# Hybrid encoder step in three-pass fp32r: projection units of 512 columns, halved first loads, gate rows spread by a DMA

## The reference, cut to what matters

```python
xn = rmsnorm(x, g);  z = xn @ w_in                    # qk, v, o, i, f, u, gv, mq, gates
mem_k, mem_v = rmsnorm(mem, g) @ w_k, rmsnorm(mem, g) @ w_v      # 256 memory rows, outputs too
h  = mlstm(silu(conv(qk)), v, i, f)                   # 4 heads, exponential gates, blocks in time
br_mlstm = (norm(h) * sigmoid(o)) @ w_br_mlstm
br_gmlp  = (gelu(u) * spatial(layernorm(gelu(gv)))) @ w_br_gmlp
br_mem   = attention(mq, mem_k, mem_v) @ w_br_mem
x  = x + (sum of sigmoid(gate_b) * br_b) @ w_out
y  = rmsnorm(x + hier_moe(rmsnorm(x)))                # top 1 of 4 groups, top 2 of 8 experts
```

## Time and profile before

| | |
|---|---|
| median of 3 runs | 876.8 us (875.28 to 878.03) |
| profiled execution | 878.86 us, span 876.9 us, mean granted clock 0.981 |
| busy | PE 847.6 us (97%), DVE 592.2 (68%), ACT 481.1 (55%), POOL 61.0 (7%) |
| DMA | 185.8 MB, 212 GB/s over the span |
| expert part | from about 575 us to the end |

### The profile page before, as it was taken

The page is one execution under the profiler, slowest core; times in us unless marked ns, Lnnn a source line. Parts: engine busy times, 40 slices in busy tenths (PEclk is TensorE's granted clock), DMA queues, the critical chain, the costliest instruction groups (busy, mean ns, idle before and its releaser), DMA issues. The chain is left out here.

```text
span 876.9 us, 12973 instructions
## 1 busy us (share of the span) xinstructions
PE 847.6 (97%) x5153; PEld 768.6 (88%) x5153; DVE 592.2 (68%) x837; ACT 481.1 (55%) x647; POOL 61.0 (7%) x126
## 2 busy tenths in 40 slices
PE   5999999999999999999999999999999999999993
PEld 5998989999989998999999998988888788878872
DVE  5665477763345536686555456379889989899883
ACT  4564467754433234454333344437777968877862
POOL 3302011020011011000000000010000000010010
PEclk9999999999999999999999999879999999999997
DMA  9757343334444434445436453559999999999960
GB/s 260 221 161 267 108 139 125 116 96 131 137 132 133 144 120 169 122 126 189 134 120 213 151 190 140 178 183 357 368 341 355 369 386 374 367 369 366 362 238 17
DMA packets 100212, 185.82 MB, mean 212 GB/s; under 512 B 5625, under 2 KB 71441, under 8 KB 100145
## 3 DMA queue, kind: packets, MB, share of 16 engines
q1 hardware_dynamic: 95280, 171.47, 57.2%
q0 software_dynamic: 4064, 11.79, 4.0%
q10 hardware_dynamic: 800, 1.66, 0.5%
HBM read 177.76 MB, written 7.92 MB: 212 GB/s over the span
## 5 line engine op out<-in xcount | busy, mean ns | idle before, releaser
L1356 DVE TENSOR_TENSOR unit_r<-arena,unit_r 128x2048 fp32r<-128x2048 f32 x63 | 144.8, 2299 | 140.8 <-ACT unit_r L966 140.6
L1365 DVE TENSOR_TENSOR w_r<-arena,w_r 128x2048 fp32r<-128x2048 f32 x96 | 217.0, 2287 | 27.9 <-ACT w_r L977 27.9
L570 PE MATMUL pj<-xn_r,unit_r 128*128 128x320 f32 x1536 | 235.0, 311 | 0.0
L570 PEld LDWEIGHTS pj<-xn_r,unit_r 128*128 128x128 f32 x1536 | 225.5, 188 | 5.7 <-issue 3.6
L874 PE MATMUL pj<-w_r,xg 128*128 128x512 f32 x768 | 192.3, 400 | 0.2 <-ACT xg L1206 0.2
L977 ACT ACTIVATE w_r<-arena 128x2048 fp32r<-128x2048 f32 x96 | 180.5, 1913 | 1.2 <-DMA arena<-in_w_exp_up 0.7
L874 PEld LDWEIGHTS pj<-w_r,xg 128*128 128x128 f32 x768 | 143.0, 190 | 31.2 <-issue 0.3
L966 ACT ACTIVATE unit_r<-arena 128x2048 fp32r<-128x2048 f32 x63 | 120.1, 1906 | 24.8 <-PE pj L570 20.0
L903 PE MATMUL pj<-w_r,hidT 128*128 128x512 f32 x384 | 93.5, 392 | 2.7 <-DVE hidT L1719 2.0
L903 PEld LDWEIGHTS pj<-w_r,hidT 128*128 128x128 f32 x384 | 71.6, 188 | 20.1 <-DVE w_r L1365 3.7
L570 PE MATMUL pj<-br_r,unit_r 128*128 128x320 f32 x384 | 59.6, 311 | 0.0
(11 more groups left out here) (359 smaller groups left out, 819.0 us busy)
## 6 DMA issues: line engine op xcount, KB each, us to landing
arena<-in_w_in SPq DMA_DIRECT2D x40, 1024.0 KB, 5.2
arena<-in_w_exp_gate SPq DMA_DIRECT2D x64, 512.0 KB, 4.8
arena<-in_w_exp_up SPq DMA_DIRECT2D x64, 512.0 KB, 6.2
arena<-in_w_exp_down SPq DMA_DIRECT2D x64, 512.0 KB, 5.4
arena<-in_w_mem_v SPq DMA_DIRECT2D x4, 1024.0 KB, 6.4
arena<-in_w_br_mem SPq DMA_DIRECT2D x4, 1024.0 KB, 4.9
arena<-in_w_br_mlstm SPq DMA_DIRECT2D x4, 1024.0 KB, 4.9
arena<-in_w_br_gmlp SPq DMA_DIRECT2D x4, 1024.0 KB, 5.0
```

What stands on the lines that cost most here:

```text
L570: last = mm(bank_of(s)[0:out_rows, 0:out_cols], l, r, start=k == 0, stop=k == len(pairs) - 1)
L1356: v.tensor_tensor(unit_r[n % RING][:, 1, :], ringw[:, n % RING, :], unit_r[n % RING][:, 0, :], ALU.subtract).then_inc(u_lo, 1)
L1365: v.tensor_tensor(w_r[u % NS][:, 1, :], raw_w[u % NS], w_r[u % NS][:, 0, :], ALU.subtract).then_inc(m_lo, 1)
```

## The change

- `memk`, `memv`, `v` and `gv` have units of 512 rows by 512 columns, still 1 MB (a third entry in `UNITS` is the half of the rows). Two units in a row, halves `kh` 0 and 1, make one output of 512 columns in one PSUM bank; behind half 0 the bank is kept (`held`) and not evacuated. Semaphore `u_half` tells ACT that a half-0 unit is used.
- The memory rows are loaded in four half tiles, units 0 and 1 in halves of 256 rows (`unit_quarters`), in the order of their use; `memk` starts with the first halves. The transposes of the second halves and `memnorm` move behind the first `memk` steps, and `xnorm`, `params`, `state`, `xT` each one or two places later. The tiles of x are loaded before and behind unit 2.
- The gain rows are loaded by ACT's queue and not by SP's.
- The gate rows are written to HBM by POOL's queue and read back to all 128 partitions (`rbb`); `bc` has no matmul.

```diff
     step("gains")
-    for i in range(2):
-        for half in range(2):
-            step("memT", i, half)
-    step("memnorm", ring=None, eng=None)
+    step("memT", 0, 0)
+    step("memT", 1, 0)
 
     xT = lambda i: lambda: (step("xT", i, 0), step("xT", i, 1))
     x_rest = lambda i: lambda: step("xrest", i, ring=None, eng=None)
-    early = [lambda: None, lambda: step("xnorm", ring=None, eng=None), lambda: step("params"), lambda: step("state"),
-             xT(0), xT(1), xT(2), lambda: None, lambda: step("gates"), lambda: (step("gates_log", ring=None, eng=None), x_rest(0)()), x_rest(1), x_rest(2),
+    early = [lambda: (step("memT", 0, 1), step("memT", 1, 1)), lambda: step("memnorm", ring=None, eng=None), lambda: step("xnorm", ring=None, eng=None), lambda: step("params"), lambda: step("state"),
+             xT(0), xT(1), xT(2), lambda: step("gates"), lambda: (step("gates_log", ring=None, eng=None), x_rest(0)()), x_rest(1), x_rest(2),
              lambda: step("gates_scan", ring=None, eng=None), lambda: step("gates_exp", ring=None, eng=None), lambda: step("wsT"), lambda: step("cols")]
-    for u in range(4):
-        n = unit("w_mem_k", u * 256)
-        for i in range(2):
-            step("memk", u, i, ring="pj", eng="A", unit=n, last=i == 1)
-            early.pop(0)()
-    for u in range(4):
-        n = unit("w_mem_v", u * 256)
-        for i in range(2):
-            step("memv", u, i, ring="pj", eng="A", unit=n, last=i == 1)
-            early.pop(0)()
+    def wide(kind, name, col, u, tiles, engs, after):
+
+        for kh in range(2):
+            n = unit(name, col + u * 512, kh)
+            for i in range(tiles):
+                step(kind, u, kh, i, ring="pj", eng=engs[i], unit=n, last=i == tiles - 1, held=kh == 0, of=(kind, u, 0, i) if kh else None)
+                after(u, kh, i)
+
+    for kind in ("memk", "memv"):
+        for u in range(2):
+            wide(kind, "w_" + kind[:3] + "_" + kind[3], 0, u, 2, "AA", lambda u, kh, i: early.pop(0)())
...
-                step("bc", c)
+                step("bc", c, ring=None, eng=None)
...
-    for u in range(4):
-        n = unit("w_in", V0 + u * 256)
-        for i in range(3):
-            step("v", u, i, ring="pj", eng="AAD"[i], unit=n, last=i == 2)
-        if u == 1:
+    for u in range(2):
+        wide("v", "w_in", V0, u, 3, "AAD", lambda u, kh, i: None)
+        if u == 0:
             step("cvT", 0, eng="A")
...
+    for u in range(2):
+        wide("gv", "w_in", GV0, u, 3, "AAD", lambda u, kh, i: event() if u + kh else None)
...
+        if _s.get("of"):
+            _s["at"] = _by_name[_s["of"]]["at"]
+            _ring_steps[_s["ring"]][_s["at"]] = _s
+        else:
+            _s["at"] = len(_ring_steps[_s["ring"]])
+            _ring_steps[_s["ring"]].append(_s)
+        if not _s.get("held"):
+            _seen[_s["ring"], _s["eng"]] += 1
+            _s["evacuated"] = _seen[_s["ring"], _s["eng"]]
...
         def _(sp):
-            for r0, name in ((P_MIX, "norm_mix_g"), (P_MEM, "mem_norm_g")):
-                sp.dma_start(prows[r0:r0 + 8, :], I[name][0, :].rearrange("(c p) -> c p", p=128)).then_inc(s_gains, 16)
+            def memory_half(i, half):
+                cs = slice(half * 512, half * 512 + 512)
+                sp.dma_start(mem_tm[:, i, cs], I["mem_prompt"][0, i * 128:(i + 1) * 128, cs]).then_inc((s_mem, s_memb)[half][i], 16)
+
+            def unit_quarters(n, half):
+                src = I["w_mem_k"][0, n * 512 + half * 256:n * 512 + half * 256 + 256, 0:512].rearrange("(k p) n -> p k n", p=128)
+                dst = ringw[:, n, half * (UW // 2):(half + 1) * (UW // 2)].rearrange("p (k n) -> p k n", n=512)
+                sp.dma_start(dst, src).then_inc(unit_full[n] if half else h_full[n], 16)
+
             for i in range(2):
-                sp.dma_start(mem_tm[:, i, :], I["mem_prompt"][0, i * 128:(i + 1) * 128, :]).then_inc(s_mem[i], 16)
-                src = I["w_mem_k"][0, i * (D // 2):(i + 1) * (D // 2), 0:256].rearrange("(k p) n -> p k n", p=128)
-                dst = ringw[:, 0, i * (UW // 2):(i + 1) * (UW // 2)].rearrange("p (k n) -> p k n", n=256)
-                sp.dma_start(dst, src).then_inc(unit_full[0] if i else u0_full, 16)
+                memory_half(i, 0)
+                unit_quarters(0, i)
+            for i in range(2):
+                memory_half(i, 1)
+            for i in range(2):
+                unit_quarters(1, i)
...
+            for n, (name, col, *part) in enumerate(UNITS):
+                if n in (RING, RING + 1):
+                    for i, (t0, rows_) in tuple(enumerate(TILES))[0 if n == RING else 1:1 if n == RING else 3]:
                         src = I["x_prompt"][0, t0:t0 + rows_, :] if i < 2 else I["x_sample"][0, :, :]
                         sp.dma_start(x_tm[0:rows_, i, :], src).then_inc(s_x, 16)
-                if n == 0:
+                if n < RING:
                     continue
                 if n >= RING:
                     sp.wait_ge(u_lo, n - RING + 1)
-                src = I[name][0, :, col:col + 256].rearrange("(k p) n -> p k n", p=128)
-                sp.dma_start(ringw[:, n % RING, :].rearrange("p (k n) -> p k n", n=256), src).then_inc(unit_full[n % RING], 16)
+                w = 512 if part else 256
+                r0 = part[0] * 512 if part else 0
+                src = I[name][0, r0:r0 + UW // w * 128, col:col + w].rearrange("(k p) n -> p k n", p=128)
+                sp.dma_start(ringw[:, n % RING, :].rearrange("p (k n) -> p k n", n=w), src).then_inc(unit_full[n % RING], 16)
...
+            def project_half(s, rows_, kh, passes, operands):
+
+                for k in range(4):
+                    for m in range(passes):
+                        l, r = operands(k, m)
+                        last = mm(bank_of(s)[0:rows_, 0:512], l, r, start=kh + k + m == 0, stop=kh == 1 and k == 3 and m == passes - 1)
+                return last
...
+                    u, kh, i = a
+                    if n < 2:
+                        pe.wait_ge(s_mnl, 2 * kh + i + 1)
+
+                    def memory_part(tile, ks):
+                        bank = bank_of(_by_name[kind, u, kh, tile])
+                        for k in ks:
+                            for m, (p, q) in enumerate(PARTS):
+                                last = mm(bank[:, 0:512], mn_r[:, p, 4 * kh + k, tile * 128:tile * 128 + 128], w[:, q, k, :], start=kh + k + m == 0, stop=kh == 1 and k == 3 and m == 2)
+                        return last
+
+                    if n < 2 and i == 0:
+                        pe.wait_ge(h_lo[n], 1)
+                        last = memory_part(0, (0, 1))
+                    elif n < 2:
+                        memory_part(1, (0, 1))
+                        pe.wait_ge(u_lo, n + 1)
+                        last = memory_part(0, (2, 3))
+                        if kh:
+                            last.then_inc(ready["pj"], 1)
+                        last = memory_part(1, (2, 3))
+                    else:
+                        last = memory_part(i, range(4))
...
-                elif kind == "bc":
-                    last = mm(b[:, 0:T + TS + 1], sel[0:H, a[0], :], rb[0:H, :], start=True, stop=True)
...
-                last.then_inc(ready[s["ring"]], 1)
+                if not s.get("held"):
+                    if (kind, a) != ("memk", (0, 1, 0)):
+                        last.then_inc(ready[s["ring"]], 1)
+                elif s["last"]:
+                    last.then_inc(u_half, 1)
...
+            for r0, name in ((P_MEM, "mem_norm_g"), (P_MIX, "norm_mix_g")):
+                act.dma_start(prows[r0:r0 + 8, :], I[name][0, :].rearrange("(c p) -> c p", p=128)).then_inc(s_gains, 16)
...
+                if n - RING in _half_units:
+                    act.wait_ge(u_half, _half_units.index(n - RING) + 1)
+                elif n >= RING:
                     act.wait_ge(ready["pj"], _last_use[n - RING] + 1)
                 af(unit_r[n % RING][:, 0, :], ringw[:, n % RING, :], ACT.Copy).then_inc(u_hi, 1)
 
-            def first_unit_high(half, signal):
+            def half_high(n, half):
                 cs = slice(half * (UW // 2), half * (UW // 2) + UW // 2)
-                af(unit_r[0][:, 0, cs], ringw[:, 0, cs], ACT.Copy).then_inc(signal, 1)
+                act.wait_ge(unit_full[n] if half else h_full[n], 16)
+                af(unit_r[n][:, 0, cs], ringw[:, n, cs], ACT.Copy).then_inc(u_hi if half else h_hi[n], 1)
...
+                elif kind == "memT":
+                    i, half = a
+                    ks, ts = slice(4 * half, 4 * half + 4), slice(i * 128, i * 128 + 128)
+                    if half and not i:
+                        half_high(1, 0)
+                    act.wait_ge(*done("memT", i, half))
+                    af(mn_r[:, 0, ks, ts], mnT[:, ks, ts], ACT.Copy).then_inc(s_mnh, 1)
+                    if not half:
+                        half_high(0, i)
+                    elif not i:
+                        half_high(1, 1)
...
```

(29 more changed lines are left out.)

142 lines of the change are left out of this document (56 added, 86 removed).

## The result

| | before | changed |
|---|---|---|
| first set of runs, median | 877.75 us | 882.81 us, ratio 1.0048 [1.0032, 1.0064] |
| the changed kernel again, with a later set of before | 878.08 us | 881.20 us, ratio 1.0024 [1.0007, 1.0042] |
| profiled execution | 878.86 us | 880.24 us |
| gates begin | 45.05 us | 51.47 us (+6.42) |
| the 16 gates matmuls, to the next group | 4.07 us | 5.83 us (+1.76) |

In the later sets three executions lay far above all others and are in no ratio: one of before at 1671 us, one of e6 at 1386 and one of e8 at 940.

The account below looks back on a forecast made before the run. PE was taken as the bound between 24 and 500 us. Gates start +3.5, gates to mq -0.7, gate rows -3.4 and wide matmuls -2.8 gave -3.4 us from the median 876.8: 873.4 us, range 867.5 to 880.

Parts of the forecast that it names:

- The gates at 48.5: Start: PE waits 2.4 us for the last x gains behind unit 5's split; gates at 48.5 instead of 45.05, +3.5 us.
- The clock at the gates: Rival, before gates: the wait there makes the clock fall a second time, price 1.5 to 2 us, about 875.1; chance 0.17.
- The base: Whole kernel: the forecast difference of -3.4 us was taken from a median of 876.8 us for the kernel before.
- unit 3 ready 34.8: Start: the ACT and DVE chain from unit 2's split readies unit 3 at 34.8 us; PE stands about 4 us.
- the row term: Behind mq's start: four bc steps of 0.84 us each leave PE where it is full, -3.4 us.
- Wide matmuls: v and gv: 256 pairs of 256-column matmuls become 512-column ones, 11 ns saved per pair, -2.8 us (-2.0 to -3.8).
- Gate rows: Units of mq: four bc matmul steps off PE, -3.4 us; rows arrive by DMA between 80.5 and 84.1, costed at 0.
- Gains in full: Rival, start: unit 3 ready at 31, no first wait or clock fall, gates at 43.3, 868.1 us; chance 0.15.
- Gate rows late: Rival, units of mq: each us of row arrival after 81.3 stands on PE; 8 us late gives 881.4; chance 0.10.
- Small pieces slow: Rival, start: 256 and 512 KB loads land 3 us later, moving everything to unit 2, 876.4 or more; chance 0.13.
- Nothing from width: Rival, wide matmuls: only 2.5 ns saved per pair, the two terms shrink by 2.8 us, 876.2; chance 0.05.
- slower: Whole kernel: the outcome that the change makes it slower, beyond the 0.3% a measurement can tell; chance 0.22.

Follow-up runs that it names:

- e6: Kernel before with only v and gv in matmuls of 512 columns: 875.64 us, ratio 0.9969 to before.
- e8: Changed kernel with 22 extra 128-column matmuls while PE waits for the gates' operand: 879.98 us, ratio 1.0014 to before.
- e1: Changed kernel with the transposes of the last (sample) tile of x one place earlier, so their gains precede unit 5's split on DVE: 873.52 us, ratio 0.9945 to before.
- e2: Changed kernel with POOL's loads let go after unit 8 instead of 4: 881.35 us, ratio 1.004 to before.
- e9: The changed kernel run once more, unaltered: 881.20 us, ratio 1.0024 to before.
- e3: Changed kernel with the memory rows' squares and scale (memnorm) ahead of the split of unit 2: 879.39 us, ratio 1.001 to before.
- e10: Changed kernel with the gate rows spread by TensorE's four copy matmuls again: 885.05 us, ratio 1.0076 to before.
- e4: Changed kernel with the sample x transposes one place earlier and memnorm ahead of unit 2's split: 870.17 us, ratio 0.9909 to before.
- e5: Kernel before with only the gate rows by POOL's two DMAs instead of matmuls: 873.89 us, ratio 0.9963 to before.
- e7: Kernel before with gate rows by DMA and 512 columns in v and gv, old start kept: 872.56 us, ratio 0.9945 to before.
- e11: Changed kernel with sample x transposes earlier, memnorm ahead of unit 2's split and POOL's loads after unit 8: 875.24 us, ratio 0.996 to before.

## Why the prediction was wrong

**The sum against the profiled execution.** Forecast 878.9 - 3.4 = 875.5, measured 880.24: 4.7 us too low. Two terms of the start make it up, 3.0 and 1.76.

- *The gates at 48.5.* This is the step that failed. "42.7 + 0.25 + evacuation 0.7 + 1.9 + 2.3 + gains 0.65" starts the split of unit 5 when ACT is free. That was right for ACT (43.6) and wrong for the unit, which landed only at 46.4: gates at 51.47, +3.0. I had asked of unit 2 when it would land, and not of unit 5. The row was in the trace of before, where ACT also waits for a `w_mem_v` unit at 45.22, with POOL's loads beside it; there it cost PE nothing, as the last gains were done at 41.0 to 43.0:

```profile
45.22 1.91 ACT L966 ACTIVATE unit_r<-arena 128x2048 fp32r<-128x2048 f32 x1 [0.59 <-DMA arena<-in_w_mem_v]
```

The change moved the gains behind that unit and so put an old, harmless lateness on the path. e1 undoes only this and gives back 7.7 to 9.3 us, the clock's share with it; e2 takes away the cause of the lateness and gives the forecast's own times up to `mq` to 0.3 us.
- *The clock at the gates.* Named as a rival (0.17, price 1.5 to 2) and not in the sum: 5.83 us for 16 matmuls instead of 4.07, +1.76, in e9 2.4. e8 shows that it hangs on the idle time. The forecast's own wait, 2.4 us, might not have brought it: behind 2.06 us in e2 the clock stayed up. It fell in all four profiles that waited 4.99 us or more (the changed kernel, e3, e9, e10), so most of this term hangs on the late unit too.
- *The base.* The median 876.8 of three runs was low; the later sets gave 877.75 to 878.50. That puts another 1 to 1.7 us on the time, not on the difference.

**What held.** First matmul 10.5 (10.58), unit 1 used up 24.5 (24.2), unit 3 ready 34.8 (34.64), the fall of the clock behind it, unit 3 and its transposes done 42.7 (42.8). The order on ACT and DVE was the right thing to read: with it mended, e4 is 3.4 us faster than e1. What e3 gained by it while unit 5 came late, 1.8 to 3.4 us in the medians, is not clear of noise. One reason in the prediction is not borne out: the first six matmuls take 2.70 us (forecast 2.6), but the windows give a granted clock of 1.00 there (10.6 to 13.2 us), and before too (11 to 14 us), so that the low clock makes them slow is not shown. (Its 1.3 us also sets a covered time, 7.15, against a distance, 5.83; with 6.00 covered it is 1.15.) From the gates' end to `mq` 20.76 us instead of 21.46: -0.70 as forecast. Between `mq` and `v` it is 4.1 us less and not 3.4, and e5 has the same 4.1 with the rows as its only change, so the row term was 0.7 too small. Most of this lies at the interruptions: 96 matmuls of `mq` with the four steps took 18.20 us before (70.58 to 88.78), and 96 without them at most 14.34 in e7, so at least 3.86 less. Wide matmuls -2.6 in the trace and -2.7 in e6 for -2.8. The Trainium skill ("TensorE: Matmul & The Clock Gate", Back-to-back issue gap) puts a single warm matmul at N/2.4 + 2.5 ns; from that I estimate 0.6 us for these 256 pairs, and the -2.7 of e6 do not agree. Gate rows: -3.4 forecast, -3.3 in e5, -3.9 in e10 by the medians. Their arrival: 8.9 us behind the first issue where I had 8 to 11.6.

**The rivals.** "Gains in full" was not this kernel, but its premise was right, and e4 is that kernel (870.2 for 868.1). "Gate rows late" did not happen in the two profiles of the changed kernel, with 0.4 us to spare in the first, but did in a profile of e7 with 3.9 us; its mechanism was right, and most of the lateness (4.0 of 4.6 us against the changed kernel) was in the small write and not in the broadcast. "Small pieces slow" did not happen: first matmul at 10.58. "Nothing from width" fell with e6.

**The chances.** I gave 0.22 to slower, and none of it to a unit that lands late. Three stages of one chain each with its own load deserved a case "a unit is not there when its engine is".

What stays open: the first median, 882.81, lies 2.6 us over its profile and 1.6 over the second median. e9's trace explains 1.4 of such a difference; the rest was in no trace.

## What to carry to other kernels

When a step moves to behind another on an in-order engine, ask of that other step both when its engine is free and when its data is there; a landing that was late and harmless before shows only as a short DMA wait on the engine that splits. Moving loads that compete takes the lateness somewhere else (e2, e11), moving the one small step that is stuck behind it cost nothing (e1). And an idle time of PE of about 2 us belongs in a sum twice, once with the clock falling behind it and once without: here it went both ways at nearly the same length.
